# Interleaving sixteen modulation slabs with the third branch's merge slabs: the order of weight reads and of the hand-written fill list changes

## The reference

```
mod    = cond @ ada_w + ada_b                 # 6*1024 columns, for two conditions
h      = rmsnorm(x) modulated by mod
proj   = h @ w_in                              # feeds four mixers and the merge gates
y_a, y_b, y_c, y_d = hyena, hgrn2, ssd, gated delta rule     # 512 wide each
mixed  = sum_n sigmoid(merge_n) * (y_n @ w_branch[n])        # n = 0..3, 1024 wide
x      = x + gate1(mod) * (mixed @ w_out)
h2     = rmsnorm(x) modulated by mod; x = x + gate2(mod) * MoE(h2)
y      = rmsnorm(x)
```

## Time and profile before

| | |
|---|---|
| time, median of 3 runs (lowest, highest) | 1378.91 us (1377.6, 1381.08) |
| the profiled execution: its time, its span | 1378.36 us, 1376.2 us |
| busy in the span: PE, DVE, ACT, POOL | 96%, 44%, 28%, 22% |
| mean granted TensorE clock | 0.995 of full speed |
| the small and dense inverse steps begin | about 538.7 us |
| "turn" 0, the last entry of the fill list, ends; first lift of the fourth branch | 698.4 us; 699.5 us |

### The profile page before, as it was taken

One profiled execution on the slowest core, in us unless ns is written; L12 is line 12 of the kernel. 1 busy time (PEld: TensorE's weight loads), 2 busy tenths in 40 slices (PEclk: granted clock), 3 DMA queues, 4 the chain that ended last, 5 costly groups with the idle time before them and its releaser, 6 DMA issues.

```text
span 1376.2 us, 20641 instructions
## 1 busy us (share of the span) xinstructions
PE 1327.2 (96%) x7692; PEld 925.8 (67%) x7692; DVE 604.7 (44%) x1363; ACT 378.9 (28%) x765; POOL 307.2 (22%) x247
## 2 busy tenths in 40 slices
PE   7999999999999998799999999999999999999996
PEld 2695899989988996588988875444544445444452
DVE  3467452886545486643232375222233323222224
ACT  3232222322544254323311241211222112211122
POOL 0431234243135553332442010000000000000001
PEclk9999999999999999999999999999999999999998
DMA  9640423133212337712335247999999999999992
GB/s 364 215 126 10 138 93 123 33 121 93 92 61 93 107 123 276 261 42 82 113 104 195 93 168 268 419 418 420 419 421 421 420 421 421 421 419 419 419 416 82
DMA packets 109744, 321.57 MB, mean 234 GB/s; under 512 B 12489, under 2 KB 72649, under 8 KB 81136
## 3 DMA queue, kind: packets, MB, share of 16 engines
q1 hardware_dynamic: 98416, 307.68, 58.4%
q0 software_dynamic: 2560, 8.81, 1.6%
q10 hardware_dynamic: 8704, 4.20, 1.1%
HBM read 320.11 MB, written 4.33 MB: 236 GB/s over the span
## 4 chain that ended last, share of the span: by engine, by line
PE 85%; DMA 9%; DVE 3%; issue 1%; ACT 1%; SPq 0%; POOL 0%; DVEq 0%; POOLq 0%; ACTq 0%
PE banks L660 24%; PE banks L627 17%; PE banks L3051 12%; DMA w<-in_exp_w 7%; PE banks L3098 7%; PE banks L2953 6%; PE banks L1067 2%; PE banks L2938 2%; PE banks L1236 2%; PE banks L2946 1%; PE banks L900 1%; PE banks L634 1%; PE banks L779 1%; PE banks L711 1%; PE banks L1295 1%
## 5 line engine op out<-in xcount | busy, mean ns | idle before, releaser
L3051 PE MATMUL banks<-w,xg 128*64 128x512 f32 (+1 forms) x1312 | 236.0, 594 | 2.1 <-DMA w<-in_exp_w 2.0
L3051 PEld LDWEIGHTS banks<-w,xg 128*64 128x64 f32 (+1 forms) x1312 | 71.9, 126 | 151.5 <-issue 125.3
L660 PE MATMUL banks<-hT,ring 128*128 128x192 f32 x888 | 154.4, 326 | 0.2 <-DMA ring<-in_w_in 0.2
L660 PEld LDWEIGHTS banks<-hT,ring 128*128 128x128 f32 x888 | 145.5, 190 | 2.8 <-DMA ring<-in_w_in 0.9
L3428 POOL DMA_INDIRECT fetched<-token_rows,row_of_place x32 | 32.1, 1004 | 443.6 <-DVE row_of_place L3229 433.5
L3098 PE MATMUL banks<-w,hidT 128*64 128x512 f32 (+1 forms) x656 | 122.8, 601 | 0.5 <-DMA w<-in_exp_w 0.3
L2953 PE MATMUL banks<-y,selT 128*128 128x512 f32 x384 | 115.0, 415 | 0.0
L660 PE MATMUL banks<-x,ring 128*128 128x192 f32 x592 | 108.8, 327 | 2.7 <-POOL ring L2582 1.7
L660 PE MATMUL banks<-x,combos 128*128 128x192 f32 x592 | 108.4, 326 | 0.7 <-ACT yT L1407 0.7
L660 PEld LDWEIGHTS banks<-x,ring 128*128 128x128 f32 x592 | 97.4, 190 | 3.4 <-issue 2.0
L660 PEld LDWEIGHTS banks<-x,combos 128*128 128x128 f32 x592 | 98.1, 190 | 1.0 <-POOL ring L2598 0.9
(11 more groups left out here) (513 smaller groups left out, 1946.2 us busy)
## 6 DMA issues: line engine op xcount, KB each, us to landing
w<-in_exp_w SPq DMA_DIRECT2D x198, 1024.0 KB, 14.0
ring<-in_w_in SPq DMA_DIRECT2D x46, 1024.0 KB, 5.4
ring<-in_ada_w SPq DMA_DIRECT2D x24, 1024.0 KB, 6.0
ring<-in_w_branch SPq DMA_DIRECT2D x8, 1024.0 KB, 5.4
ring<-in_w_out SPq DMA_DIRECT2D x4, 1024.0 KB, 6.8
arena<-in_sh_w SPq DMA_DIRECT2D x3, 1024.0 KB, 8.0
x<-in_x_sample SPq DMA_DIRECT2D x4, 512.0 KB, 8.4
token_rows<-whole_rows SPq DMA_DIRECT2D x3, 384.0 KB, 21.7
```

What stands on the lines that cost most here:

```text
L660: last = mm(out, lhsT=w[:, k, :], rhs=tokens[:, k, :], start=start and k == 0, stop=k == KD // 2 - 1, skip_group_check=not start)
L3051: ins = mm(ps[lo:hi, :], lhsT=xg[:, k, a_ * P + lo:a_ * P + hi], rhs=w13[:, a_, u, :, k, :], start=k == 0, stop=k == KD - 1)
```

## The change

The sixteen slabs of modulation groups 1 and 2 stood in one block of the plan, ahead of the third branch's merge and branch slabs (`plan_lift(2)`). Now the six slabs of the third branch and the two slabs of `gdn_g` stand between them. The fill tables are rewritten in the same order: the merge pairs and lifts of the third branch begin in the small levels, the modulation slabs of group 2 are used one by one until the "end", and the columns of group 2 are turned there. VectorE's split of the second gate's columns into two parts (`mod_parts`) moves behind the "end", the matmul engine's wait for it behind the lifts of the fourth branch, and ScalarE waits for group 1's columns where it waited for group 2's.

```diff
         DELTA_FILL = {
-            "start": (("ada", 1, 3, 5), ("q_norms",), ("values",)),
-            ("c", 1): (("ada", 1, 5, 6),),
-            ("c", 2): (("ada", 1, 7, 8),),
-            ("c", 3): (("ada", 2, 1, 2),),
-            ("c", 4): (("ada", 2, 3, 4),),
-            (0, 5): (("ada", 2, 5, 6),),
-            (0, 6): (("ada", 2, 6, 8), ("scaled_values",), ("combine", 2, 0)),
-            (1, 5): (("ada_columns", 2), ("open", 2, 0), ("residual", 0, FWD), ("residual", 0, BWD)),
-            (1, 6): (("solve", 1, FWD), ("lift", 0), ("lift", 1), ("open", 2, 1)),
-            (2, 5): (("state", FWD), ("close", 2, 1)),
-            (2, 6): (("open", 2, 2), ("solve", 2, FWD), ("solve", 2, BWD)),
-            "end": (("close", 2, 2), ("state", BWD), ("lift", 4), ("lift", 5), ("residual", 1, BWD), ("open", 2, 3),
-                    ("query_rows",), ("close", 2, 3), ("solve", 1, BWD), ("lift", 6), ("lift", 7), ("combine_gate", 0),
-                    ("open_gate", 0), ("solve", 0, FWD), ("solve", 0, BWD), ("close_gate", 0), ("out", 1), ("open_gate", 1),
-                    ("out", 2), ("close_gate", 1), ("out", 0), ("last_state",), ("combine", 3, 0), ("open", 3, 0),
-                    ("turn", 1), ("turn", 2), ("close", 3, 0), ("turn", 0))}
+            "start": (("combine", 2, 0), ("q_norms",), ("values",), ("ada", 1, 3, 4)),
+            ("c", 1): (("open", 2, 0),),
+            ("c", 2): (("ada", 1, 5, 6), ("lift", 0)),
+            ("c", 3): (("open", 2, 1),),
+            ("c", 4): (("lift", 2), ("lift", 3)),
+            (0, 5): (("open", 2, 2),),
+            (0, 6): (("ada", 2, 2, 3), ("lift", 4), ("scaled_values",)),
+            (1, 5): (("residual", 0, FWD), ("residual", 0, BWD), ("lift", 5), ("ada", 2, 3, 4)),
+            (1, 6): (("solve", 1, FWD), ("close", 2, 3), ("ada", 2, 4, 5), ("combine_gate", 0)),
+            (2, 5): (("state", FWD), ("lift", 6)),
+            (2, 6): (("solve", 2, FWD), ("solve", 2, BWD), ("ada", 2, 5, 6)),
+            "end": (("state", BWD), ("ada", 2, 6, 7), ("open_gate", 0), ("residual", 1, BWD), ("close_gate", 0), ("ada", 2, 7, 8),
+                    ("query_rows",), ("solve", 1, BWD), ("solve", 0, FWD), ("solve", 0, BWD), ("ada_columns", 2),
+                    ("open_gate", 1), ("out", 1), ("close_gate", 1),
+                    ("out", 2), ("combine", 3, 0), ("open", 3, 0), ("out", 0), ("last_state",), ("turn", 1), ("turn", 2),
+                    ("close", 3, 0), ("turn", 0))}
         DELTA_AFTER = {
-            ("c", 1): (("ada", 1, 6, 7),),
-            ("c", 2): (("ada_columns", 1), ("ada", 2, 0, 1)),
-            ("c", 3): (("ada", 2, 2, 3),),
-            ("c", 4): (("ada", 2, 4, 5),),
-            (0, 5): (("keys_to_end",),),
-            (1, 5): (("close", 2, 0),),
-            (2, 5): (("lift", 2), ("lift", 3), ("residual", 1, FWD))}
+            ("c", 1): (("ada", 1, 4, 5), ("close", 2, 0)),
+            ("c", 2): (("lift", 1), ("ada", 1, 6, 7)),
+            ("c", 3): (("ada", 1, 7, 8), ("close", 2, 1)),
+            ("c", 4): (("ada_columns", 1), ("ada", 2, 0, 2)),
+            (0, 5): (("keys_to_end",), ("close", 2, 2)),
+            (1, 5): (("open", 2, 3),),
+            (2, 5): (("lift", 7), ("residual", 1, FWD))}
...
-        plan_ada(1)
-        plan_ada(2)
-        plan_lift(2)
-        plan("gdn_g")
+        plan_ada(1, 0, 4)
+        plan_merge(2, 0)
+        plan_ada(1, 4, 6)
+        plan_branch(2, 0)
+        plan_ada(1, 6, 7)
+        plan_merge(2, 1)
+        plan_ada(1, 7, 8)
+        plan_ada(2, 0, 2)
+        plan_merge(2, 2)
+        plan_ada(2, 2, 3)
+        plan_branch(2, 1)
+        plan_ada(2, 3, 4)
+        plan_merge(2, 3)
+        plan_ada(2, 4, 7)
+        plan("gdn_g", 1)
+        plan_ada(2, 7, 8)
+        plan("gdn_g", 2, 1)
         plan_lift(3)
...
-            pe.wait_ge(s_row_parts.sem, 1)
             lift(3, 0, 2, merged=True)
             for h in (1, 2, 3):
                 pair("merge", 3, h)
                 lift(3, 2 * h, 2 * h + 2, merged=True)
 
+            pe.wait_ge(s_row_parts.sem, 1)
...
-                    banks.emptied(act, ("adaT", 2))
+                    banks.emptied(act, ("adaT", 1))
...
+            fill("end")
             lane.link(v.tensor_copy(mod_parts[:, 0], mod[:, 40:48, :]))
             s_row_parts.on(tt(mod_parts[:, 1], mod[:, 40:48, :], mod_parts[:, 0].bitcast(F32), ALU.subtract))
-            fill("end")
```

More of the change, by code:

```diff
@@ L534, in trunk, with plan_ada, plan @@
         slab_plan = []
-        def plan_ada(group):
-            for k in range(KD):
+        def plan_ada(group, lo=0, hi=KD):
+            for k in range(lo, hi):
                 slab_plan.append((("ada", group, k), ada[k * P:(k + 1) * P, None, group * 2048:(group + 1) * 2048]))
         plan_ada(0)
-        def plan(name, halves=2):
-            for h in range(halves):
+        def plan(name, halves=2, first=0):
+            for h in range(first, halves):
                 slab_plan.append(((name, h), cols_of(w_in, COL[name] + h * 256)))
@@ L546, in plan_merge, with plan_branch @@
             slab_plan.append((("merge", n, h), cols_of(w_in, COL["merge"] + n * D + h * 256)))
+        def plan_branch(n, h):
+            slab_plan.append((("wb", n, h), a["w_branch"][0, n][:, h * W:h * W + W].rearrange("(k p) n -> p k n", p=P)))
         def plan_lift(n, first=0):
@@ L552, in plan_lift @@
                 if h % 2 == 0:
-                    slab_plan.append((("wb", n, h // 2), a["w_branch"][0, n][:, h // 2 * W:h // 2 * W + W]
-                                      .rearrange("(k p) n -> p k n", p=P)))
+                    plan_branch(n, h // 2)
         for name in ("hy_v", "hy_x1", "hy_x2"):
```

## The result

The changed kernel is slower: 1402.99 us median (1401.19 to 1405.57, 4 runs) against 1379.14 (1377.6 to 1381.08, 4 runs), a ratio of 1.0174 with a 95% interval of 1.0153 to 1.0194. Slower was forecast, at 1391.8 within 1380 to 1397; the time lies above the range, and the loss, 23.9 us, is nearly twice the 12.9 that the sum gave.

A forecast was written before the change was run, and what follows sets the result against it. The matmul engine was taken to bound the kernel, idle for 18.0 us between 523 and 700. Idleness after, 3.2 + 6.9 + 4.9 + 14.8 + 1.1 = 30.9 us, gave +12.9: 1391.8 us, range 1380 to 1397.

The forecast's parts named there:

- the sum: Matmul engine, 523 to 700: idle time 30.9 us after the change against 18.0 before, so 12.9 us slower.
- The gain of the small levels: Delta inverse, levels 1 to 3: pairs and lifts fill the steps, no wait, no 1.8 us gaps before the small inverses.
- the branch slab that holds back SP until the last lift: Level 4: branch slab 7, held from lift 0 to lift 3, keeps SP at slab 11 until 580.0.
- The three new waits: Matmul engine stalls of 6.9 us in level 4, 4.9 in tile 0 and 14.8 in tiles 1 and 2.
- the one before slab 11: Level 4: 4.6 us for modulation slab 11, 1.6 for slab 12, 0.7 for merge slab 13; 6.9 us in all.
- the first: Wait before the first small products, for VectorE: grows from 2.3 to 3.2 us.
- the second stall: Tile 0: GpSimd's keys queue behind its combine of merge slab 3; the matmul engine waits 4.9 us.
- one dip before and one after: Matmul engine's clock: one 1.7 us dip each before and after, so no net cost; two after would make 14.6 us.
- contention: GpSimd beside VectorE: early combine of merge 0 delays VectorE by at most 1.3 us; stalled combines at most 1.1 each.
- At nothing: Moved second gate split, ScalarE's wait and group 2 columns lie under other work; the split uncovered would cost 0.4 us.
- fast one: Whole kernel: gate's combine holding nobody, 1379.5 us, chance 0.08; all slabs in time, 1365 us, chance 0.10.
- The gate's combine holds nobody: Tiles 1 and 2: matmul engine stops 2.8 us instead of 14.8; 1379.5 us, no change; chance 0.08.

The follow-up runs named there:

- experiment 1: Changed kernel with GpSimd's combine for the first gate slab moved behind the masked keys, into step (2, 6): 1389.68 us, ratio 1.0084 to the kernel before.
- experiment 2: On top of experiment 1, GpSimd's combine of merge slab 3 moved behind its keys, into step (0, 6): 1378.79 us, ratio 1.0002 to the kernel before.
- experiment 4: Changed kernel with useless matmuls put ahead of four of its waits, nothing removed: 1393.74 us, ratio 1.0113 to the kernel before.
- experiment 5: Changed kernel with useless matmuls before its largest wait's end only: twenty over the wait, 1399.64 us; four after the gate slab lands, 1398.91 us.
- three_late: Changed kernel with the GpSimd moves of experiment 1, experiment 2 and experiment 3 together: 1376.06 us, ratio 0.9986 to the kernel before.
- experiment 3: Changed kernel with GpSimd's first combine of the third branch waiting for VectorE's first masked copy: 1398.62 us, ratio 1.0138 to the kernel before.
- experiment 7: Kernel before with only the late group 2 columns and the moved waits and splits of the change: 1379.74 us, ratio 1.0004.
- experiment 8: Kernel before with useless matmuls in gaps of its inverse, before the small inverses, gprod(0, 5) and ginv(0, 5): 1380.03 us, ratio 1.0009.

## Why the prediction was wrong

*Direction and mechanism: right.* The gain of the small levels came, the branch slab that holds back SP until the last lift was right, and so was GpSimd's program, in which the keys of the dense steps queue behind a `combine` that waits for a slab. Experiments 1 and 2 show the two GpSimd stalls apart, each by moving one entry. The three new waits came in the forecast order, two of them within 1 us (14.9 for 14.8, 5.9 for 4.9); the one before slab 11 was shorter, 4.2 instead of 6.9: its first slab landed 4.9 us after its start instead of 5.9, and the merge slab behind was no longer waited for. The total of idleness, 31.6 for 30.9, was right, but in part by luck: this wait was 2.7 shorter than forecast, the first 1.8 longer, the second stall 1.0 longer, and the 0.7 on ScalarE stayed.

*The term that failed: the clock.* The sum said one dip before and one after, 1.7 us each, and allowed one more. Four dips came, and the two longest cost 2.8 and 2.9. They make 8.4 us more than before, where the sum had nothing and its upper bound 1.7. Experiment 4 shows it: 9.2 us come back by useless work alone (7.8 in the profiled delta stretch); experiment 5 shows 3.4 us behind the largest wait. The 11.6 us by which the span's 24.5 exceed the forecast 12.9 are 8.4 of clock, 0.7 of idleness, 1.5 of work in shorter turns and 1.0 from the start of the run. I had read the price off one dip of the kernel before, which follows gaps of 2 us with work between, and set one dip for any wait. The waits forecast were four, of 3.2, 6.9, 4.9 and 14.8 us, and the row on the clock should have been applied behind each. The Trainium skill, "TensorE: Matmul & The Clock Gate", Part 1, was cited for two dips; what its rule says, the lower clock behind an idle array until it has worked again, holds here behind each of the four waits, whose longest parts were 4.8, 3.7, 5.9 and 14.9 us; it did not show behind the 2.9 us wait of `three_late`, where the clock stayed at 1.00.

*A second term at nothing.* "No matmul is added or removed" was right, but the sum took from it that their time stays the same. In shorter turns they took 1.5 us more.

*A bound that failed: contention.* The early first `combine` was allowed to delay VectorE by one GpSimd operation, 1.3 us. It took 1.9 (experiment 3): by their times the two masked copies lie beside GpSimd's three sums (535.9 to 539.9) and are stretched by them, while the sums keep their 1.3 us each. "SBUF — State Buffer", Who interferes with whom, in the Trainium skill says that two SBUF inputs on VectorE and a GpSimd read exclude each other for an operation; the trace agrees, for a masked copy (2.95 us for the two beside the sums, 1.01 without). As a share of the miss it is small.

*At nothing: right.* The late columns (experiment 7).

*The rivals.* Neither fast one came. "The gate's combine holds nobody" would have been 1379.5; experiment 1, which makes it true, gives 1389.7, since the other stalls stay with their clock: that rival's time, too, lacked the clock. (By its own idle time of 18.9 us it should have read 1379.8.)

*The range.* Its bounds of 9.7 and 19.6 us give 1388.6 and 1398.5, not the 1387 and 1397 that were set beside them. The measured 1403 lies above either.

*Open:* whether the shorter turns make all of the 1.5 us, and the part of experiment 3's median that its trace doesn't show. For the latter there is a lead, not a proof: how long the dip behind a short wait lasts, or whether there is one, differs between executions (below).

## What to carry to other kernels

When work is put into a hand-written fill list, follow every engine's own order, not only that of the engine which is to be filled: an entry that is harmless to one can make another wait for a transfer with small, urgent work queued behind. Moving two such entries of GpSimd was worth 24 us here and made the same idea level with the kernel before; with the first combine behind the masked copy and the slabs in the order of first need as well, it became 0.3% faster. Price each forecast wait of the matmul engine twice, once for the wait and once for the work behind it at the lower clock (less where that work is followed by a wait for a transfer anyway, experiment 4). Where a gap can't be closed, a few useless matmuls at its end bring the clock back in time; they gave nothing on the kernel before, where a gap behind them stayed unfilled.

## What the runs showed of the hardware

The granted clock is back after four slow matmuls in the last 5 us of a 14.9 us wait, and that is worth as much (1398.9 us) as twenty over the whole wait (1399.6). Filling the gaps up to 571 did not rid the kernel before of its one dip: it lay at 571 to 575 in its own profile, and behind 577.8 in experiment 8 and, unfilled, in experiment 7. A pair of masked copies on VectorE took 2.95 us beside GpSimd's adds and 1.01 without.

The same wait does not always cost the clock the same. Behind the 4.8 us before the first small products the two profiled kernels of experiments 1 and 2, which are the same up to there, lost 1.7 and 3.0 us to the lower clock. Experiment 3 and `three_late` have the same 2.9 us there, and again the same program up to there; experiment 3, at 537 to 540,

```profile
537.00:540.00 3.00, 2.25 (x22) 1.91 (x26) 2.97 (x6) 0.87 (x3) 2.84 (x3) 0.50 0.99 317
```

runs at the lower level behind it, and `three_late` keeps the upper one:

```profile
540.00:544.00 4.00, 4.00 (x45) 3.80 (x38) 3.87 (x7) 0.89 (x3) 2.99 (x3) 1.00 0.53 186
```
